# Two value products and two identity products of a scan inverse moved into the first pass of a loop, under a branch on the loop counter

## The reference, cut to what matters

```python
def wkv7_scan(r, w, k, v, a, b):
    B, T, H, N = r.shape                     # T = 272, H = 16 heads, N = 64
    xs = tuple(jnp.moveaxis(t.astype(jnp.float32), 1, 0) for t in (r, w, k, v, a, b))

    def step(S, inp):
        r_t, w_t, k_t, v_t, a_t, b_t = inp
        sa = jnp.einsum("bhij,bhj->bhi", S, a_t)
        S = S * w_t[:, :, None, :] + sa[..., None] * b_t[:, :, None, :] + v_t[..., None] * k_t[:, :, None, :]
        y = jnp.einsum("bhij,bhj->bhi", S, r_t)
        return S, y

    S0 = jnp.zeros((B, H, N, N), jnp.float32)
    _, ys = lax.scan(step, S0, xs)
    return jnp.moveaxis(ys, 0, 1).astype(r.dtype)
```

## Time and profile before

| what | value |
|---|---|
| median of 3 runs | 1574.82 us |
| range of the runs | 1570.5 to 1585.86 us |
| the profiled execution, its own time | 1575.16 us |
| its span, first to last instruction | 1573.4 us |
| PE busy | 1534.5 us, 98% of the span |
| mean granted TensorE clock | 0.991 |
| the scan's stretch | 330 to 454 us |

### The profile page before, as it was taken

The page is one execution under the profiler, slowest core; times in us unless marked ns, Lnnn a source line. Parts: engine busy times, 40 slices in busy tenths (PEclk is TensorE's granted clock), DMA queues, the critical chain, the costliest instruction groups (busy, mean ns, idle before and its releaser), DMA issues.

```text
span 1573.4 us, 40624 instructions
## 1 busy us (share of the span) xinstructions
PE 1534.5 (98%) x16097; PEld 1472.5 (94%) x16097; DVE 664.0 (42%) x1608; ACT 780.6 (50%) x1289; POOL 1139.9 (72%) x860
## 2 busy tenths in 40 slices
PE   6999999999899999999999999999999999999998
PEld 6999999878899999999999998699999998899998
DVE  4334568764546333223332148743342336452200
ACT  5444557632345544445444443754445545665432
POOL 6876757983528878778877784178878985488885
PEclk9999999998899999999999999999999999999999
DMA  7544543320023544455544552055545553245551
GB/s 271 187 164 152 168 164 135 107 69 2 2 83 108 181 166 162 148 200 186 186 146 156 196 176 81 2 209 204 187 137 183 188 182 108 87 158 192 183 185 79
DMA packets 37908, 231.30 MB, mean 147 GB/s; under 512 B 4527, under 2 KB 6680, under 8 KB 16552
## 3 DMA queue, kind: packets, MB, share of 16 engines
q1 hardware_dynamic: 36552, 228.57, 41.5%
q10 hardware_dynamic: 1248, 1.24, 0.2%
HBM read 228.67 MB, written 2.63 MB: 147 GB/s over the span
## 4 chain that ended last, share of the span: by engine, by line
PE 72%; DVE 2%; issue 1%; ACT 1%; POOL 1%; SPq 0%; DMA 0%; DVEq 0%; POOLq 0%; ACTq 0%
PE PS L843 58%; PE PS L842 1%; PE PS L1107 1%; PE PS L1114 1%; PE PS L1122 1%; PE PS L1528 1%; POOL wlo L797 1%; PE PS L1146 1%; PE PS L1152 1%; PE PS L1304 0%; ACT whi L2788 0%; PE PS L1097 0%; PE PS L1296 0%; DMA raw<-w_f_in_in 0%; PE PS L1514 0%
## 5 line engine op out<-in xcount | busy, mean ns | idle before, releaser
L797 POOL TENSOR_TENSOR wlo<-raw,whi 128x256 fp32r<-128x256 f32 (+1 forms) x754 | 1072.7, 1454 | 336.7 <-ACT whi L2788 314.7
L843 PE MATMUL PS<-xh,whi 128*128 128x272 f32 (+1 forms) x2304 | 665.9, 289 | 19.2 <-POOL wlo L797 16.4
L843 PE MATMUL PS<-xl,whi 128*128 128x272 f32 (+1 forms) x2304 | 657.5, 285 | 0.0
L843 PE MATMUL PS<-xh,wlo 128*128 128x272 f32 (+1 forms) x2304 | 656.9, 285 | 0.0
L2788 ACT ACTIVATE whi<-raw 128x1024 fp32r<-128x1024 f32 x468 | 455.4, 982 | 353.5 <-PE PS L843 332.4
L843 PEld LDWEIGHTS PS<-xh,whi 128*128 128x128 f32 x2304 | 433.3, 188 | 28.7 <-issue 19.7
L843 PEld LDWEIGHTS PS<-xl,whi 128*128 128x128 f32 x2304 | 434.6, 189 | 0.5
L843 PEld LDWEIGHTS PS<-xh,wlo 128*128 128x128 f32 x2304 | 435.0, 189 | 0.0
L843 PE MATMUL PS<-hid_h,whi 128*128 128x272 f32 (+1 forms) x960 | 273.7, 285 | 2.1 <-POOL wlo L797 1.6
L843 PE MATMUL PS<-hid_h,wlo 128*128 128x272 f32 (+1 forms) x960 | 273.7, 285 | 0.0
L843 PE MATMUL PS<-hid_l,whi 128*128 128x272 f32 (+1 forms) x960 | 272.8, 284 | 0.0
(11 more groups left out here) (436 smaller groups left out, 1627.7 us busy)
## 6 DMA issues: line engine op xcount, KB each, us to landing
raw<-w_f_in_in SPq DMA_DIRECT2D x88, 1024.0 KB, 4.8
raw<-w_f_dn_in SPq DMA_DIRECT2D x64, 704.0 KB, 4.1
raw<-w_b_ff_in SPq DMA_DIRECT2D x32, 1024.0 KB, 4.8
raw<-w_rk_k_in SPq DMA_DIRECT2D x4, 1024.0 KB, 4.9
raw<-w_rk_r_in SPq DMA_DIRECT2D x4, 1024.0 KB, 5.1
raw<-w_rk_v_in SPq DMA_DIRECT2D x4, 1024.0 KB, 5.4
raw<-w_rk_o_in SPq DMA_DIRECT2D x4, 1024.0 KB, 5.3
raw<-w_at_q_in SPq DMA_DIRECT2D x4, 1024.0 KB, 5.0
```

The lines of the kernel that those rows point to most:

```text
L797: last = nc.gpsimd.tensor_tensor(wlo[U % SPL][:, piece], raw[U % RAW][:, piece], whi[U % SPL][:, piece].bitcast(F32), ALU.subtract)
L843: mm(out, a, b, start=start and n == 0, stop=stop and n == 2, **kw)
```

## The change

For each half, PE's last two value products (`lak_v` of pairs c0 + 2 and c0 + 3) and the identity products of pairs 2 and 3 leave the straight code ahead of the loop. They now stand in the loop's body behind the `level_update` of pair 0, under a branch that is taken into them in the first pass only (`pe.If(lv < 1)`). The two value products wait there for ACT's copies of the level products whose banks they overwrite (`s_qc`), the wait for their own copies (`s_p1c`) stands at the end of the body, and the loop's start waits for `c0 + 2` of these copies and for the token copies. On ACT the two `lak_v_copy` stand behind the four copies of level 0. DVE, POOL and SP keep their order. Nothing is padded: the code that follows is shifted by the few instructions that the branch and the waits add.

```diff
@@ PE
                 grams_b(c0 + 3, 0)
                 pe.wait_ge(s_p1c, c0 + 2)
                 grams_a(c0 + 3, 2)
-                pe.wait_ge(s_tka, 2 * c0 + 7)
-                lak_v(c0 + 2, 4)
-                pe.wait_ge(s_ga, c0 + 4)
-                pe.wait_ge(s_tka, 2 * c0 + 8)
-                lak_v(c0 + 3, 6)
                 pe.wait_ge(s_gb, c0 + 4)
-                for p in range(4):
+                for p in range(2):
                     pe.wait_ge(s_xd, 16 * half + p + 1)
                     inverse_in(p)
-                pe.wait_ge(s_p1c, c0 + 4)
+                pe.wait_ge(s_tka, 2 * c0 + 8)
+                pe.wait_ge(s_p1c, c0 + 2)
                 with link.loop(4, 0) as lv:
                     for p in range(4):
                         pe.wait_ge(s_lm, val(16 * half + p + 1, lv, 4))
@@
                         pe.wait_ge(s_xd, val(16 * half + p + 1, lv, 4))
                         pe.nop(nofuse=True)
                         level_update(p)
+                        if p == 0:
+                            with pe.If(lv < 1):
+                                pe.wait_ge(s_ga, c0 + 4)
+                                for q in (2, 3):
+                                    pe.wait_ge(s_xd, 16 * half + q + 1)
+                                    inverse_in(q)
+                                pe.wait_ge(s_qc, 16 * half + 2)
+                                lak_v(c0 + 2, 4)
+                                pe.wait_ge(s_qc, 16 * half + 4)
+                                lak_v(c0 + 3, 6)
+                    pe.wait_ge(s_p1c, c0 + 4)
                 pe.wait_ge(s_xb, c0 + 1)
                 uz_product(c0, 4)
@@ ACT
-                lak_v_copy(c0 + 2, 4)
-                lak_v_copy(c0 + 3, 6)
                 for lv in range(4):
                     for p in range(4):
                         act.wait_ge(s_q, 16 * half + 4 * lv + p + 1)
                         f(qq[p][:, :], PS[0:BLK, 4 + p, 0:192], ACT.Copy).then_inc(s_qc, 1)
+                    if lv == 0:
+                        lak_v_copy(c0 + 2, 4)
+                        lak_v_copy(c0 + 3, 6)
```

## The result

Over 19 runs of each on one chip, the kernel before took 1574.82 us (median; 1570.5 to 1585.86) and the changed one 1612.37 us (1577.58 to 1617.76). The forecast was 1574.9 us with a range up to 1582, so it was wrong: the change costs some 2.4% by the medians. The ratio to before is 1.0059 [1.0038, 1.008], but it leaves out runs more than 1.5% above a kernel's fastest, which 12 of the changed kernel's 19 are (1611 to 1618 us, mean granted clock .96; of the others four took 1586 to 1591 us at .98 and three 1578 to 1580 us at .99), so the median tells of the usual run and the ratio does not. The profiled execution took 1591.35 us, 16.2 us more than the one of before.

A forecast was written before the change was run, and what follows sets the result against it. PE, busy nearly all the span, was taken as the bound. First half 0 and second half -0.3 us on the profiled 1575.16 us gave 1574.9 us, range 1567 to 1582 us.

The forecast's parts named there:

- Part 1: Ahead of the loop: value products leave, PE waits 0.95 us for the first mask, the loop starts 2.6 us earlier.
- Part 3: Fetch gaps in the first pass: first half's moves to the level products, 1.7 us; second half's two become one, 1.5 us.
- no gain in the first half: First half's loop: the moved fetch gap leaves the second pass starting at 357.3 us, against 357.36 before.
- rival C: In the loops the clock stays at 2.4 GHz: 4.2 us gained a half, 8.4 in both, 1566.5 us; chance 0.09.
- Part 2: First pass: moved products add 2.9 us; the branch costs 0 to 0.27 us a pass, taken as 0.1 in the first.
- rival E: In one half the clock stays low one stretch longer because of the new gaps: +4.2 us, 1579.1 us; chance 0.08.
- D: In the loop, instruction blocks are fetched anew every pass if PE holds only four: +22 us (1597) or +56 (1631); chance 0.08.

The follow-up runs named there:

- emptyif: The kernel before with an empty branch on the loop counter (only a no-operation under it) behind the update of pair 0, in mid-pass: 1600.14 us, ratio 1.0177.
- endif: The kernel before with an empty branch on the loop counter behind the update of pair 3, at the pass's end: 1575.81 us, ratio 1.0011.
- aligned2: The changed kernel with padding at the head of each half, so both loops start at slot 80 of a 16 KB block: 1571.23 us, ratio 0.9985.
- late_dup: The kernel before with value products of pairs 2 and 3 made again under a branch behind the update of pair 3: 1585.36 us, ratio 1.0075.

## Why the prediction was wrong

Part 1 held. The first half of this execution lies about 1 us later than forecast and the second about 2 us earlier (first identity product at 404.10, and 348.05 + 58.3 = 406.35 by the forecast), so I compare distances from the first identity product of each half. Forecast: loop after 0.75 us (348.05 to 348.8); measured 0.83 (349.11 to 349.94). The wait for the mask was put at 0.95 us and is 1.00.

Part 3 held for the gaps. Forecast: one at the end of line 1107's products in each half, 1.7 and 1.5 us, after 131 and 142 products; measured 1.49 and 1.67 us, after 132 and 141. Second pass of the first half 9.25 us behind the first identity product, measured 9.28. In the second half 10.4 to 10.7, measured 11.46: the clock fell 6.3 us behind the first identity product (410.4) where I had it 6.85 behind, so the 24 records of value products took 3.42 us (409.85 to 413.27), where I had 3.1, and the updates behind them 0.3 us more; the rest is the longer gap and small terms. Those are sizes, not mechanisms. But "no gain in the first half" did not hold: with no fall of the clock there, its loop ended 2.3 us ahead of before's, which is rival C in one half.

Part 2's branch price was mis-sized where the clock is full. I took 0 in passes two and three, because PE runs behind its stream there; that holds at 1.2 GHz only (5.41 us in emptyif against 5.35 before). At 2.4 GHz the passes of the changed kernel take 4.14 and 4.04 us (358.39 to 362.53 to 366.57) instead of 3.67, so 0.4 to 0.5 us each, above my bound of 0.27. Over two halves that is 1 to 3 us, next to a loss of 37.

The step that failed is what the sum holds at nothing and rival E at "+4.2": that the clock comes back in the passes as it did before, one stretch of 13.6 us later at the most. I took the return from the earlier trace rows as a property of the passes, and never asked what in them brings it back or whether the branch breaks that. The low clock lasted 58 us in one half, or 126 in both, ran through the work behind the loop, and cost 15.8 us there in the profiled execution and some 32 in the one at 1617.25 us.

The profiled executions of the changed kernel, of before and of the ten experiments that edit one of them have 26 first passes, and they order the causes:

- What comes before a fall. In 19 first passes stands a gap of 1.09 us or more. In 17 of them the clock fell in or behind a gap; in one it fell ahead of it (endif, second half), in one it did not fall (the changed kernel, first half). In the seven with no gap or one of at most 0.44 us, the clock did not fall in the loop. That the place of the code decides is shown by aligned2 against the changed kernel, and the gap is what the place changed in the loops; that a gap isn't the only thing, endif shows. Nor is any idle time enough: all 13 profiled executions have 1.7 us of it near 241 us, between large products of line 843, and only emptyif shows a fall there (242.1 to 245.5).
- What keeps it down. Eight of the 18 falls came with a branch in mid-pass, and in all eight the clock came back only behind the loop, 24 to 65 us later. Ten came with no branch or one at the pass's end, and in all ten it was back before the loop ended, after 3.4 to 17 us. That the place of the branch does it is shown by emptyif against endif.
- Without a fall the mid-pass branch does no harm beyond its 0.4 to 0.6 us a pass (aligned2).

The range had no place for this. D, my only large loss, was about fetches in every pass, and q8's 73 packets and passes without gaps refute it: one packet left at 358.95 and the next at 374.40, behind the loop. PE must hold the five blocks that D named. By that, the trace also disagrees with the two-block store of the Trainium skill's page "Runtime: NRT & Kernel Launch" (instruction fetch mechanics), as I had taken it. C was right as a possibility (no fall in the first half of the profiled execution), but each of its passes then paid for the branch.

What stays open: why a branch in the middle of a pass keeps the clock at 1.2 GHz and one at its end doesn't. Idle time of PE is not the answer: at half clock a pass with the branch in the middle shows none and stays slow, while late_dup's passes show 0.3 us each (5.67 us, 366.74 to 372.41) and the clock returns. What differs is that the level products run unbroken over a whole pass in one (288 records) and in runs of 180 and 108 in the other. Whether the break must be a branch wasn't tried. Open too is what decides, from run to run, whether the clock falls at all: four of 25 runs of the changed kernel took 1580 us or less, one of them 1567.75 us.

## What to carry to other kernels

When a change puts a branch or anything else that breaks the stream into a dense loop of small products, ask what the loop did for the clock: look up where the granted clock comes back, and price the case in which it doesn't, over all of the work behind it. Try the same edit at the other end of the loop's body. A hole in instruction fetch is cheap by its own length (1.5 us) and dear by the fall of the clock that follows it; it can be hidden under slow products if the bounds of the 16 KB blocks fall on them. Padding sets the bounds, but it shifts all of the code behind it and can open a gap elsewhere (2.12 us at 450.17 in aligned2), and right in front of the loop it left a gap of 1.60 us in one of two halves. Read the mean granted clock of every run, not of one profile alone: for the changed kernel it goes from .96 to .999.

## What the runs showed of the hardware that I had not expected

- At 2.4 GHz a branch on the loop counter costs PE 0.3 us a pass at the end of the body (3.97 us against 3.67) and 0.4 to 0.6 in the middle (4.04, 4.14 and 4.23). In the middle it shows as longer products and as no idle time; at the end it shows as idle time (0.54 us ahead of the next pass against 0.27). At 1.2 GHz it costs 0.3 us at the end (5.67 us in late_dup against 5.35) and 0.06 to 0.17 in the middle (5.41 in emptyif, 5.48 and 5.52 in the changed kernel at 1617.25 us).
- The same empty branch, moved by three updates, changed the whole kernel by some 26 us: 1600.14 against 1573.84 for before on one chip, 1575.81 against 1576.05 on another.
- Once down, the clock of the changed kernel stayed at 1.2 GHz for 58 to 65 us with PE busy nearly all the time (64.25 of 64.70 us).
- In the scan's small products a gap in instruction fetch (1.09 to 3.71 us) came with a fall of the clock in most of the profiled cases, in the loops (17 of 19) and behind them (five of six, 450.17 in aligned2 for one), and a gap of at most 0.44 us in none. Between the large products of line 843, 1.7 us of idle time near 241 us came with one in 1 of 13.
